# Differential attention on one Trainium2 core: POOL adds the two weighted maps of a pair before the turn

## What is computed

```python
def differential_attention(q, k, v, slopes, lam):      # H = 4 heads, 2 maps each, E = 64
    for each block i of Q_BLOCK = 128 queries:
        s = einsum('bqhce,bkhce->bhcqk', q_block, k) * E ** -0.5
        s = where(dist >= 0, s - slope * dist, NEG_INF)
        p = softmax(s, axis=-1)
        attn = p[:, :, 0] - lam * p[:, :, 1]
        out = einsum('bhqk,bkhe->bqhe', attn, v)        # v is 2 * E = 128 wide
```

## Time and profile before

| | us |
|---|---|
| three runs | 3038.51, 3034.48, 3037.96 |
| median | 3037.96 |
| the profiled execution: span from the first to the last instruction | 3034.8 |
| of it, differential heads, from the turn of t1 of the first to the last value product | 1995.2 to 2035.7 |
| PE busy in the span | 2984.2 (98%) |
| POOL busy in the span | 1454.2 (48%) |

### The profile page before, as it was taken

The page is one execution under the profiler, slowest core; times in us unless marked ns, Lnnn a source line. Parts: engine busy times, 40 slices in busy tenths (PEclk is TensorE's granted clock), DMA queues, the critical chain, the costliest instruction groups (busy, mean ns, idle before and its releaser), DMA issues.

```text
span 3034.8 us, 40195 instructions
## 1 busy us (share of the span) xinstructions
PE 2984.2 (98%) x14440; PEld 2413.2 (80%) x14440; DVE 1164.0 (38%) x2004; ACT 1293.5 (43%) x2025; POOL 1454.2 (48%) x843
## 2 busy tenths in 40 slices
PE   8999999999989999999999989999999999999999
PEld 7886787888878777787888878778888887788887
DVE  5344333221053444334222070554555128455510
ACT  4455445222244455445223253664444237444431
POOL 4555455444445655455444445554444444344443
PEclk9999999999999999999999999999999999999999
DMA  4222242333322122233333323203333333233333
GB/s 140 65 83 77 70 125 91 96 95 99 104 90 91 57 90 70 73 122 102 97 97 98 108 79 97 63 1 97 97 97 96 96 93 96 83 96 95 96 96 97
DMA packets 80296, 274.34 MB, mean 90 GB/s; under 512 B 8744, under 2 KB 14504, under 8 KB 80176
## 3 DMA queue, kind: packets, MB, share of 16 engines
q1 hardware_dynamic: 75120, 266.05, 28.4%
q10 hardware_dynamic: 5056, 6.63, 0.7%
HBM read 270.54 MB, written 2.10 MB: 90 GB/s over the span
## 4 chain that ended last, share of the span: by engine, by line
PE 93%; DVE 3%; ACT 1%; issue 1%; POOL 1%; DMA 0%; SPq 0%; DVEq 0%; ACTq 0%
PE ps L666 24%; PE ps L668 23%; PE ps L667 23%; PE ps L928 3%; PE ps L939 2%; PE ps L962 2%; PE ps L1157 1%; PE ps L1158 1%; PE ps L1163 1%; PE ps L1317 1%; PE ps L1316 1%; PE ps L1315 1%; PE ps L746 1%; PE ps L957 1%; PE ps L1052 1%
## 5 line engine op out<-in xcount | busy, mean ns | idle before, releaser
L2589 POOL TENSOR_TENSOR WLO<-WRAW,WHI 128x1024 fp32r<-128x1024 f32 x467 | 1123.8, 2409 | 1257.0 <-ACT WHI L1366 1257.0
L666 PE MATMUL ps<-HH,WHI 128*128 128x512 f32 x2184 | 858.8, 393 | 1.2 <-POOL WLO L2589 0.9
L668 PE MATMUL ps<-HH,WLO 128*128 128x512 f32 x2184 | 850.5, 389 | 0.0
L667 PE MATMUL ps<-HL,WHI 128*128 128x512 f32 x2184 | 850.0, 389 | 0.0
L1366 ACT ACTIVATE WHI<-WRAW 128x1024 fp32r<-128x1024 f32 x467 | 490.7, 1052 | 330.2 <-DMA WRAW<-wall 329.6
L666 PEld LDWEIGHTS ps<-HH,WHI 128*128 128x128 f32 x2184 | 410.1, 188 | 89.7 <-issue 5.8
L668 PEld LDWEIGHTS ps<-HH,WLO 128*128 128x128 f32 x2184 | 409.9, 188 | 86.5
L667 PEld LDWEIGHTS ps<-HL,WHI 128*128 128x128 f32 x2184 | 410.3, 188 | 84.1 <-issue 1.0
L2446 DVE SCALAR_TENSOR_TENSOR ps<-U,COLS,ps 128x512 f32<-128x512 f32 x192 | 145.0, 755 | 121.0 <-ACT ps L1790 106.9
L2028 DVE TENSOR_TENSOR ACC<-ACC,SQ 128x512 f32<-128x512 f32 x80 | 70.5, 881 | 290.8 <-ACT SQ L1629 276.5
L1790 ACT ACTIVATE ps<-U,COLS 128x512 f32<-128x512 f32 x96 | 75.1, 783 | 157.5 <-DVE U L2145 157.5
(11 more groups left out here) (382 smaller groups left out, 4874.1 us busy)
## 6 DMA issues: line engine op xcount, KB each, us to landing
WRAW<-wall SPq DMA_DIRECT2D x502, 512.0 KB, 3.5
DFT<-dft ACTq DMA_DIRECT2D x4, 516.0 KB, 5.5
XROWS<-xin SPq DMA_DIRECT2D x4, 512.0 KB, 7.9
y<-YROWS ACTq DMA_DIRECT2D x8, 256.0 KB, 2.0
PROWS<-pin ACTq DMA_DIRECT2D x2, 512.0 KB, 3.9
DIL<-dil ACTq DMA_DIRECT2D x1, 768.0 KB, 4.1
COLS<-cols ACTq DMA_DIRECT2D x1, 290.5 KB, 6.2
POSI<-posi SPq DMA_DIRECT2D x1, 256.0 KB, 9.0
```

Source lines behind the costliest of these rows:

```text
L666: pe.matmul(out_, WHI[w_at], x_hi, start=first, stop=False)
L667: pe.matmul(out_, WHI[w_at], x_lo, start=False, stop=False)
L668: return pe.matmul(out_, WLO[w_at], x_hi, start=False, stop=last)
L2589: pool.tensor_tensor(WLO[:, s, :], whole, WHI[:, s, :].bitcast(F32), ALU.subtract).then_inc(wt_lo, 1)
```

## The change

It concerns the 16 differential pairs alone. POOL still multiplies each of the two maps by its column of RS, and now counts `probs_weighted` for that. Then it waits for its own two results and adds the second map to the first (a new TENSOR_TENSOR), and that counts `probs_ready`. From there on there is one map: PE turns one, ACT copies one, and PE multiplies one by the values. Maps are therefore no longer numbered 2 q + c: `maps_of`, `maps_before` and `pair_of_map` count 2 for a dilated pair and 1 for a differential one, and the bank of a turn is that number modulo 2. Dilated pairs and the other attentions do what they did.

```diff
+        single = DIFF_H * ST if mode == "banded" else 0
+        per = {k: n for k in ("scores_ready", "exp_ready")}
+        per |= {k: n - single for k in ("probs_ready", "probs_turned", "turned_copied")} | ({"probs_weighted": 2 * single} if single else {})
...
+        def maps_of(st, q):
+            return 1 if differential(st, pairs_of(st)[q][0]) else 2
+
+        def maps_before(st, q):
+            alone = DIL_H // 2 * ST if st.mode == "banded" else st.heads * ST
+            return q + min(q, alone)
...
             def turn(st, q):
-                for c in range(2):
-                    n = 2 * q + c
+                for c in range(maps_of(st, q)):
+                    n = maps_before(st, q) + c
...
             def value_products(st, q):
                 if differential(st, g):
-                    for c in range(2):
-                        for kt in range(a, b):
-                            mm = pe.matmul(out_bank(st, g)[:, at], values(st, g, c, kt), turned_at(st, 2 * q + c)[:, (kt - a) * P:(kt - a + 1) * P],
-                                           start=kt == a and c == 0, stop=kt == b - 1 and c == 1, skip_group_check=True)
+                    for kt in range(a, b):
+                        mm = pe.matmul(out_bank(st, g)[:, at], values(st, g, 0, kt), turned_at(st, m)[:, (kt - a) * P:(kt - a + 1) * P],
+                                       start=kt == a, stop=kt == b - 1, skip_group_check=True)
...
             def turned_copies(st, q):
-                for c in range(2):
-                    n = 2 * q + c
+                for n in range(m, m + maps):
...
                     if q >= 3:
-                        dve.wait_ge(S["probs_turned"], st.at("probs_turned", n - 6 + 1))
+                        dve.wait_ge(S["probs_turned"], st.at("probs_turned", maps_before(st, q - 3) + min(c + 1, maps_of(st, q - 3))))
...
             def probs_scaled(st, q):
+                both, done = [probs_at(st, q, c)[:, 0:(b - a) * P] for c in range(2)], "probs_ready"
                 if differential(st, g):
-                    pool.wait_ge(S["lambda_applied"], st.at("lambda_applied", q - DIL_H // 2 * ST + 1))
+                    n, done = q - DIL_H // 2 * ST, "probs_weighted"
+                    pool.wait_ge(S["lambda_applied"], st.at("lambda_applied", n + 1))
...
                 for c in range(2):
-                    p, s = probs_at(st, q, c)[:, 0:(b - a) * P], 2 * (q % 3) + c
-                    pool.tensor_scalar(p, p, RS[:, s:s + 1], 1.0, ALU.mult, ALU.mult).then_inc(S["probs_ready"], 1)
+                    s = 2 * (q % 3) + c
+                    pool.tensor_scalar(both[c], both[c], RS[:, s:s + 1], 1.0, ALU.mult, ALU.mult).then_inc(S[done], 1)
+                if differential(st, g):
+                    pool.wait_ge(S["probs_weighted"], st.at("probs_weighted", 2 * n + 2))
+                    pool.tensor_tensor(both[0], both[0], both[1], ALU.add).then_inc(S["probs_ready"], 1)
```

More of the change, by code:

```diff
@@ L293, in attention @@
         n = 2 * pairs
-        per = {k: n for k in ("scores_ready", "exp_ready", "probs_ready", "probs_turned", "turned_copied")}
+        single = DIFF_H * ST if mode == "banded" else 0
+        per = {k: n for k in ("scores_ready", "exp_ready")}
+        per |= {k: n - single for k in ("probs_ready", "probs_turned", "turned_copied")} | ({"probs_weighted": 2 * single} if single else {})
         per |= {k: pairs for k in ("neg_max_ready", "inverse_ready", "pair_multiplied")}
@@ L554, in differential, with pair_of_map @@
             return st.mode == "banded" and g >= DIL_H // 2
+        def maps_of(st, q):
[3 more added lines that the diff above has]
+            return q + min(q, alone)
+        def pair_of_map(st, n):
+            alone = DIL_H // 2 * ST if st.mode == "banded" else st.heads * ST
+            return n // 2 if n < 2 * alone else n - alone
         def pairs_of(st):
@@ L938, in turn @@
                     for k in range(b - a):
-                        mm = pe.transpose(turn_ps[c][:, k * P:(k + 1) * P], probs_at(st, q, c)[:, k * P:(k + 1) * P], IDENT[:, :])
+                        mm = pe.transpose(turn_ps[n % 2][:, k * P:(k + 1) * P], probs_at(st, q, c)[:, k * P:(k + 1) * P], IDENT[:, :])
                     mm.then_inc(S["probs_turned"], 1)
@@ L944, in value_products @@
                 a, b = spans(st.mode, t)
-                pe.wait_ge(S["turned_copied"], st.at("turned_copied", 2 * q + 2))
+                m = maps_before(st, q)
+                pe.wait_ge(S["turned_copied"], st.at("turned_copied", m + maps_of(st, q)))
                 if t == 0:
@@ L961, in value_products @@
                         for c in range(2):
-                            mm = pe.matmul(out_bank(st, g)[half(c), at], values(st, g, c, kt), turned_at(st, 2 * q + c)[:, (kt - a) * P:(kt - a + 1) * P],
+                            mm = pe.matmul(out_bank(st, g)[half(c), at], values(st, g, c, kt), turned_at(st, m + c)[:, (kt - a) * P:(kt - a + 1) * P],
                                            start=kt == a, stop=kt == b - 1, skip_group_check=True)
@@ L1586, in exponentials @@
                 if mode == "mla" and q >= 3:
-                    act.wait_ge(S["probs_turned"], st.at("probs_turned", 2 * (q - 3) + 2))
+                    act.wait_ge(S["probs_turned"], st.at("probs_turned", maps_before(st, q - 2)))
                 for c in range(2):
@@ L1597, in turned_copies @@
                 slots = 4 if carried(st) else TURNED
-                if 2 * q >= slots:
-                    act.wait_ge(S["pair_multiplied"], st.at("pair_multiplied", (2 * q - slots) // 2 + 1))
-                for c in range(2):
-                    n = 2 * q + c
+                m, maps = maps_before(st, q), maps_of(st, q)
+                if m + maps > slots:
+                    act.wait_ge(S["pair_multiplied"], st.at("pair_multiplied", pair_of_map(st, m + maps - 1 - slots) + 1))
+                for n in range(m, m + maps):
                     act.wait_ge(S["probs_turned"], st.at("probs_turned", n + 1))
-                    act.activation(turned_at(st, n)[:, 0:(b - a) * P], turn_ps[c][:, 0:(b - a) * P], ACT.Copy).then_inc(S["turned_copied"], 1)
+                    act.activation(turned_at(st, n)[:, 0:(b - a) * P], turn_ps[n % 2][:, 0:(b - a) * P], ACT.Copy).then_inc(S["turned_copied"], 1)
             def attention(st):
```

## The result

The changed kernel is slower: 3045.59 us median of 11 runs (3043.41 to 3048.14) against 3037.5 for the kernel before in 11 runs. The medians are 8.1 us apart, and the ratio of the runs, with its 95% interval, is 1.0029 [1.0021, 1.0037]. The forecast was 3040. The measured median lies inside the stated range (3034.5 to 3046), at its slow end, where the rival of the clock had put 3043 to 3049. The profiled execution has a span of 3044.4, 9.6 over that of the kernel before.

A forecast was written before the change was run, and what follows sets the result against it. PE bounds the kernel now; afterwards the round through all engines does. First head +1.6, two steady heads +0.25 and tail +0.25 sum to +2.1 on 3037.96, giving 3040 us, range 3034.5 to 3046.

The forecast's parts named there:

- the rival of the clock: PE idling in the changed heads drops its clock to 1.2 GHz: once +3, each head +9, 3043 to 3049; chance 0.15.
- the mean of the changed head, 70%: PE's expected busy share over a changed head, held against the 50% before the earlier clock fall.
- (b): From PE's turn of t1 to that of t3: 5.9 us, 5.6 without DVE's wait for POOL's add.
- (a): From PE's turn of t3 to that of the next t1, through scores, DVE and POOL: 4.9 us.
- The round: Chain through all four engines from turn to turn, with POOL's add in full: 10.7 us a head; chance 0.62.
- The estimate in proportion: POOL's add of 512 scaled from the skill page's 4497 ns for 2048 elements: 1.12 us; set aside for the row's 1.29.
- The wait of RS by LS: In t3, DVE's multiplication stands still until POOL's add ends; without this the sum would be 0.3 us a head less.
- the rival that its 0.17 made of it: DVE's NM waits behind POOL's adds, holding up the inverse: 0.6 to 1.2 us a head more, 3042 to 3044; chance 0.17.
- First head and tail: First head +1.6 us, POOL reaching its weight remainder later; tail, last turn of t1 to end of products, +0.25.
- no change: The expected outcome: a difference from the kernel before within 0.2% or 6.1 us; chance 0.81.
- PE's saving: Fewer value products and transposes on PE: 3.3 us a head, from 10.58 to 7.3, turning into waiting for `probs_ready`.

The follow-up runs named there:

- filled: Changed kernel with PE repeating the value products of t0 nine times and of t1 three times, output unchanged: 3038.15 us, 1.0004 of the kernel before.
- no add: Changed kernel without POOL's add: both maps weighted, only the first turned and multiplied, second missing from the output: 3031.27 us, 0.9981 of the kernel before.
- one DVE operation: Changed kernel with POOL out of the differential pairs: DVE joins both maps in one instruction, first map's 1 / s0 left out: 3029.71 us, 0.9974.

## Why the prediction was wrong

**The step that failed** is the rival of the clock, and in it one reading: "Against: the mean of the changed head, 70%, lies above the 50% that went before the fall." The mean over a head was the wrong thing to hold against a stretch of 4.00 us. The head's idle time isn't spread: all of it, 3.04 us, lies in two waits behind t0 and t1, where PE's pieces are smallest, and there PE was busy 1.96 of 4.00, next to the 1.99 of the earlier trace rows. The rival had even named the place (about half of the time around the turn of t2), and its chance of 0.15 set that aside. The fall came in every head, where the range had allowed for two in all.

**What it cost.** The rival said 2 to 3 us a head, "each head +9", and was right in size. Changed less filled: 1.15, 2.60, 2.98 in the heads and 1.65 in the tail, 8.38 in all. Its "every PE record twice as long" stands in no row; the scores here show 1.8 times. In the second head (b) is 6.08 for the forecast's 5.9: the fall comes at its end. (a) is 7.42 for 4.9. The turn of t3 takes 0.5 more (1.04 to the scores), the scores of t2 with their reads 0.75 more, and the last 1.24 are PE itself, late with t3's scores and t2's values when POOL is done.

**The round** was right. At full clock it was 5.96 + 4.94 = 10.90 in one head and 10.56 in the other, forecast 10.7. POOL's add was estimated at 0.45, 0.7, 1.0 and 1.29 and measured 0.45, 0.73, 0.99 and 1.26. The estimate in proportion, 1.12 for the widest, would have made POOL's head 0.6 shorter, not the 0.4 of the prediction; it entered no sum.

**The wait of RS by LS** was seen rightly. DVE's timeline of the changed kernel, first and second head:

```profile
2002.46 2.20 DVE L2283 TENSOR_TENSOR RS<-RS,LS 128x2 f32<-128x2 f32 x1
...
2012.17 0.72 DVE L2283 TENSOR_TENSOR RS<-RS,LS 128x2 f32<-128x2 f32 x1
...
2014.95 0.77 DVE L2274 TENSOR_SCALAR NM<-MX 128x2 f32<-128x2 f32 x1
```

The second ends at 2012.89, when POOL's add does (2011.89 + 0.99), and the first with a weight remainder. It was sized wrongly, though: 0.3 forecast, about 0.1 by the run that took it away. NM met the adds as well, once a head (0.77 in the changed, 0.78 in the filled kernel); at full clock the head stayed within 10.9, so it was not the rival that its 0.17 made of it. Why an instruction with a single input stands still as well, no row shows.

**First head and tail**: +1.6 forecast, +0.71 at full clock (11.84 for 11.13), +1.86 with the fall. The tail +0.25 forecast, -0.06 at full clock (7.92 for 7.98, to the first row of L666 or L682), +1.59 with the fall. The sum of the full clock terms is +0.95 for +2.1, and that kernel measured 0.8 over the one before. Had the clock held, the answer "no change" would have been right.

**PE's saving.** 3.3 us a head would be 7.3 for PE; PE was busy 7.50 in the steady heads of the two kernels without filling that kept their clock all through the stage (no add, one DVE operation). That it would turn into waiting was right. What the waiting then does to the clock was the term to price.

## What to carry to other kernels

When a change takes work off the engine that bounds the kernel, lay out where its idle time will fall, and compare the emptiest stretch, not the mean of the loop, with the stretch before which the trace shows the clock falling. That is a sign and no rule: the clock once held over 1.43 of 4.00 us and once fell behind 4.00 of 4.00. An operation that lies in the round from one turn to the next costs time there, though its engine is idle half of the time: the adds cost 2.1 us a head at full clock. What pays is to shorten the round (one instruction on one engine, 7.3 us faster here), not to move a part of it to another queue. If a stage must wait, repeated matmuls in the gap can be worth their while: they gave back 7.4 us here, which only brought the changed kernel level with the one before, and nothing that can be told where the clock had not fallen.

## What the runs showed of the hardware

The longest wait of PE in the changed head is 2.04 us, and the clock fell all the same. The Trainium skill, page TensorE: Matmul & The Clock Gate, section HAM oscillation, tells of long waits for a transfer that throttle the array, and its section A second HAM failure mode of short ones between groups of matmuls, which lower the throughput while the median matmul keeps its length. The rows here are nearer to the second kind, but behind each fall the matmuls themselves are longer, the scores of t3 2.08 for 1.13.

A TENSOR_SCALAR on POOL is longer with a second column as its scalar than with a constant: two of 128 x 512 take 1.52 for 1.36, 0.08 each. And DVE's SCALAR_TENSOR_TENSOR with two tiles as inputs stands still under a POOL instruction like the TENSOR_TENSOR of the earlier trace rows, 2.82 us on a map of 512 under a remainder of 2.34, where it takes 0.75 when free.
